# One decoder layer on one core: value slots a mix tile sooner, pairs of key pages summed on ScalarE, and five small steps moved

## What is computed

```
z  = x @ w_in                      columns q | k | v | B | C | h, 512 each
attention (8 heads x 64): block-sparse, ALiBi, over q, k, v
short convolution (512 channels): B * dwconv3_causal(C * h)
x1 = LayerNorm(alpha * x + concat(attn, conv) @ w_out)
u  = dwconv3_causal(x1 @ w_ffn_up);  a, g = split(u)
y  = LayerNorm(alpha * x1 + (silu(a) * g) @ w_ffn_down)
```

```
page_sum = sum over a page of cache_k[page_table]      -> block means -> gate -> top 3 blocks
p = softmax(q . k / 8 - slope * distance), other blocks masked;   out = p @ v
```

## Time and profile before

| | |
|---|---|
| median of three runs | 437.73 us |
| profiled execution | 437.8 us, its span 436.0 us |
| mean granted TensorE clock | 0.993 |
| TensorE busy | 412.7 us (95%) |
| VectorE busy | 294.7 us (68%) |
| ScalarE busy | 181.4 us (42%) |
| GpSimd busy | 110.8 us (25%) |
| DMA moved | 124.60 MB |

### The profile page before, as it was taken

The page is one execution under the profiler, slowest core; times in us unless marked ns, Lnnn a source line. Parts: engine busy times, 40 slices in busy tenths (PEclk is TensorE's granted clock), DMA queues, the critical chain, the costliest instruction groups (busy, mean ns, idle before and its releaser), DMA issues.

```text
span 436.0 us, 8237 instructions
## 1 busy us (share of the span) xinstructions
PE 412.7 (95%) x2903; PEld 339.2 (78%) x2903; DVE 294.7 (68%) x382; ACT 181.4 (42%) x694; POOL 110.8 (25%) x133
## 2 busy tenths in 40 slices
PE   4999999999999998999999989999999999999990
PEld 4588887876876774765653479999999999999990
DVE  0498999999799976954541275666776776534437
ACT  1587569644469133112110243554455555233201
POOL 1005334995255152200000717122211220000002
PEclk9999999999999999999999999999999999999997
DMA  8999999899999999999999953665556766676002
GB/s 313 397 359 407 405 407 393 316 404 409 409 359 327 338 404 405 406 405 404 402 405 398 318 196 98 194 191 162 158 169 191 213 181 186 183 211 206 3 2 99
DMA packets 109515, 124.60 MB, mean 286 GB/s; under 512 B 5903, under 2 KB 67048, under 8 KB 109466
## 3 DMA queue, kind: packets, MB, share of 16 engines
q1 hardware_dynamic: 101138, 107.30, 70.2%
q10 hardware_dynamic: 8336, 16.78, 10.2%
HBM read 121.65 MB, written 2.61 MB: 285 GB/s over the span
## 4 chain that ended last, share of the span: by engine, by line
PE 64%; DVE 18%; DMA 5%; issue 5%; SPq 4%; POOL 2%; ACT 1%; DVEq 0%; POOLq 0%; ACTq 0%
PE ps L1821 12%; PE ps L1822 11%; PE ps L1823 11%; PE ps L1714 8%; PE ps L1608 6%; DVE qk L939 6%; DVE T L949 5%; PE ps L1437 4%; PE ps L1632 4%; PE ps L1634 3%; PE ps L1384 3%; SPq L360 2%; DMA wring<-in_cache_v 2%; DMA KV<-in_cache_k 2%; POOL x1l L612 1%
## 5 line engine op out<-in xcount | busy, mean ns | idle before, releaser
L1188 DVE TENSOR_TENSOR wlo<-KV,whi 128x2048 fp32r<-128x2048 f32 (+1 forms) x24 | 61.7, 2571 | 57.5 <-ACT whi L838 29.3
L1437 PE MATMUL ps<-xT,wring 128*128 128x264 f32 x384 | 89.6, 388 | 0.1
L1437 PEld LDWEIGHTS ps<-xT,wring 128*128 128x128 f32 x384 | 71.6, 190 | 13.6 <-issue 1.7
L1821 PE MATMUL ps<-x1h,whi 128*128 128x264 f32 x256 | 73.7, 288 | 0.2
L1822 PE MATMUL ps<-x1l,whi 128*128 128x264 f32 x256 | 72.7, 284 | 0.0
L1823 PE MATMUL ps<-x1h,wlo 128*128 128x264 f32 x256 | 72.6, 284 | 0.0
L939 DVE TENSOR_TENSOR qk<-KV,qk 128x1536 f32<-128x1536 f32 (+1 forms) x32 | 67.0, 2097 | 6.6 <-DMA KV<-in_cache_k 2.7
L669 ACT ACTIVATE qk<-qk 128x64 f32<-128x64 f32 x216 | 51.9, 245 | 29.1 <-POOL qk L560 23.1
L949 DVE TENSOR_REDUCE T<-qk 128x24 f32<-128x1536 f32 (+1 forms) x32 | 58.4, 1827 | 0.0
L1821 PE MATMUL ps<-fh,whi 128*128 128x264 f32 x176 | 50.4, 286 | 0.1
L1822 PE MATMUL ps<-fl,whi 128*128 128x264 f32 x176 | 50.0, 284 | 0.0
(11 more groups left out here) (215 smaller groups left out, 574.0 us busy)
## 6 DMA issues: line engine op xcount, KB each, us to landing
KV<-in_cache_k SPq DMA_DIRECT2D x128, 256.0 KB, 6.2
KV<-in_w_ffn_up SPq DMA_DIRECT2D x32, 512.0 KB, 4.7
KV<-in_cache_v SPq DMA_DIRECT2D x60, 256.0 KB, 7.3
wring<-in_cache_v SPq DMA_DIRECT2D x56, 256.0 KB, 6.4
KV<-in_w_ffn_down SPq DMA_DIRECT2D x8, 1408.0 KB, 6.3
wring<-in_w_in ACTq DMA_DIRECT2D x5, 2048.0 KB, 14.0
zbuf<-in_cache_v SPq DMA_DIRECT2D x12, 256.0 KB, 5.3
zbuf<-in_w_ffn_up SPq DMA_DIRECT2D x3, 1024.0 KB, 10.2
```

The source lines that it names most:

```text
L1188: nc.vector.tensor_tensor(wlo[s][:, 0:n], w2[s][:, 0:n], whi[s][:, 0:n], ALU.subtract).then_inc(s_lo, 1)
L1437: ins = nc.tensor.matmul(ps[:, z_bank(n), 0:R], tile[k], xT[:, k, :], start=k == 0, stop=k == KT - 1)
L1821: nc.tensor.matmul(out, wh[k], xh[k], start=k == 0, stop=False)
```

## The change

Seven edits, each in the order or in the share of work of an engine:

- TensorE: `penalties(0)` stands in the middle of `z_tile(19)`, not ahead of it.
- TensorE: `values(0, 0)` stands ahead of the four transposes for the convolution's tail. Each later value slot up to `values(1, 3)` stands one mix tile sooner.
- GpSimd: page 17 is multiplied before the fourth convolution tile, not behind all four.
- VectorE: `multiply(20)` stands ahead of `denominators(0)`, and `scan(19)` becomes `reduce(19)`.
- Slots 22, 24, 26 and 28: VectorE sums two pages, not three, and ScalarE sums two, not one. The third page's products are VectorE's, so ScalarE can begin with them when VectorE's multiplication is done. VectorE's multiplications of slots 24, 26, 28 and 30 now also wait for ScalarE's sums of two slots before.
- SyncE: value slot 9 is fetched after the keys of sample 7's third group and a block of w_ffn_up, not before them.
- ScalarE: the copy `kv_rows(0)` stands ahead of `head_exp(0)`.

```diff
+HALVED = (22, 24, 26, 28)
@@ SyncE
             load_values(8, ids_v)
-            load_values(9, ids_v)
             load_keys(7, 2, ids_k)
             load_quad(1)
+            load_values(9, ids_v)
             load_keys(7, 3, ids_k)
@@ GpSimd
             for t in range(4):
+                if t == 3:
+                    multiply_page(17)
...
-            multiply_page(17)
             multiply_page(18)
@@ ScalarE, sum_products(j)
-                if j in POOLED:
-                    act.wait_ge(s_kpool, pool_pages(j + 1))
-                else:
-                    act.wait_ge(s_kused, j + 1)
-                for h in range(NH):
-                    x = prod[:, j % 2, GD * DA + h * DH:GD * DA + (h + 1) * DH]
...
+                for g in range(2 if j in HALVED else GD, GP):
+                    if g == GD and j in POOLED:
+                        act.wait_ge(s_kpool, pool_pages(j + 1))
+                    else:
+                        act.wait_ge(s_kused, j + 1)
+                    for h in range(NH):
+                        x = prod[:, j % 2, g * DA + h * DH:g * DA + (h + 1) * DH]
...
@@ ScalarE
+            kv_rows(0)
             head_exp(0)
-            kv_rows(0)
@@ VectorE, multiply(j) and reduce(j)
-                    if j not in POOLED:
+                    if j not in POOLED or j - 2 in HALVED:
                         dve.wait_ge(s_reda, act_sums(j - 1))
...
-                n = GP if j in WHOLE else GD
+                n = GP if j in WHOLE else 2 if j in HALVED else GD
@@ VectorE
             reduce(18)
+            multiply(20)
             denominators(0)
...
-            scan(19)
+            reduce(19)
@@ TensorE
-            penalties(0)
-            z_tile(19)
+            z_tile(19, lambda: penalties(0))
...
+            values(0, 0)
+            pe.wait_ge(s_ch, 4)
+            pe.wait_ge(s_hoc, 4)
+            for t in range(4):
+                ins = turn(ps[0:NTAIL, 3, t * P:(t + 1) * P], zT[:, 20 + t, TAIL:R])
+            ins.then_inc(s_ctps, 1)
             pe.wait_ge(s_wom, 16)
...
-            values(0, 0)
+            values(0, 1)
             mix_tile(0)
...
```

More of the change, by code:

```diff
@@ L1590, in _ @@
             head_outputs(3)
-            pe.wait_ge(s_ch, 4)
-            pe.wait_ge(s_hoc, 4)
-            for t in range(4):
-                ins = turn(ps[0:NTAIL, 3, t * P:(t + 1) * P], zT[:, 20 + t, TAIL:R])
-            ins.then_inc(s_ctps, 1)
             def values(b, s):
@@ L1656, in _ @@
             pe.wait_ge(s_ze, 24)
-            values(0, 0)
+            values(0, 1)
             mix_tile(0)
+            values(0, 2)
             mix_tile(1)
-            values(0, 1)
+            values(0, 3)
             mix_tile(2)
-            values(0, 2)
+            values(1, 0)
             mix_tile(3)
@@ L1665, in _ @@
             first_row_tile(0)
-            values(0, 3)
+            values(1, 1)
             mix_tile(4)
@@ L1669, in _ @@
             first_row_tile(2)
-            values(1, 0)
+            values(1, 2)
             mix_tile(5)
@@ L1673, in _ @@
             sample_outputs(0)
-            values(1, 1)
             mix_tile(6)
             first_row_tile(4)
-            values(1, 2)
+            values(1, 3)
             mix_tile(7)
@@ L1680, in _ @@
             first_row_tile(6)
-            values(1, 3)
             first_row_tile(7)
```

2 lines of the change are left out of this document (1 added, 1 removed).

## The result

| kernel | median of runs | ratio to before, 95% interval |
|---|---|---|
| before | 437.82 us (11 runs, 436.78 to 439.15) | 1 |
| changed | 438.73 us (11 runs, 437.74 to 440.26) | 1.0026, 1.0016 to 1.0037 |

The change makes the kernel 0.9 us longer by the medians; the ratio is estimated from all runs and puts it at 1.1 us, 0.7 to 1.6. The forecast was 436.5 us, with a range of 435.3 to 438.0: wrong in its sign, and outside its range.

The account below looks back on a forecast made before the run. The prediction took TensorE's list up to the last value slot at 239.40 us as the bound, with at most 1.42 us of DMA waits to win. +0.15 - 1.42 = -1.27 us gave 436.5 us, range 435.3 to 438.0.

Parts of the forecast that it names:

- term B: TensorE's waits for late value slots from 220 us on: all three go, -1.42 us, bounds 0 and -1.42.
- 2.0 us of lead stay: DMA behind the mix stretch: slot 20's latency of 6.2 us less slot 2's 4.2 was taken as lasting lead.
- reading M: Experiments' reading: slot 31 lands at slot 19's landing + 34.2 us or slot 20's issue + 38.4, whichever is later.
- term A: How much later TensorE leaves the mix stretch and row statistics: +0.15 us, bounds -0.24 and +2.4.
- waits for values 5 and 6: TensorE's mix stretch: value slots wanted a mix tile earlier are waited for, 0.2 us each, 0.4 us in all.
- take the place: Page 17 earlier on GpSimd: +0.3 us at 106 us, replacing the 0.4 us of waiting for values, adding nothing.
- Rival 1: Mix stretch: values arrive too late at a slower DMA rate, so the kernel is slower, 438.6 us; chance 0.13.
- rival 3: End of the value slots: the DMA's lead is lost, no waits go, 437.95 us; chance 0.15.
- the penalties' wait: TensorE's 0.86 us wait in the z tiles moves to the transpose of the maxima: 0, bounds 0 and -0.86.
- VectorE's new wait for ScalarE at slot 24: Multiplication of slot 24 waits for ScalarE's slot 22 until 133.6, ahead of its old time: 0 on the path.
- waits for the DMA at the end: Sign that the forecast is wrong: TensorE still waits for the DMA at the end; the forecast had none from 220 us.

Follow-up runs that it names:

- the block that fills the gap: Changed kernel with the 1 MB feed-forward weight block issued behind value slot 19, not slot 24: 436.92 us, 0.9979 of before.
- the control without a gap: Kernel before with the 1 MB feed-forward weight block issued behind value slot 19, not slot 24: 438.17 us, 1.0005 of before.
- the hole opened in the kernel before: Kernel before with two feed-forward half products put ahead of value slots 14 to 16 on TensorE: 444.88 us, 1.0162 of before.
- The same kernel without the block: Changed kernel with page 17, the four waits and values(1, 3) moved back, weight block still behind slot 24: 437.24 us, 0.9993 of before.
- the kernel with fillers: Kernel before with two keep_clock filler products (1.44 us) behind early_half(0, 0) on TensorE, run again: 439.72 us, one run.

## Why the prediction was wrong

- **The term B, -1.42 us, is the step that failed: "So 6.2 - 4.2 = 2.0 us of lead stay".** I read slot 20's latency against slot 2's and called the difference lead, to be used up at the end. By reading M the end of the profiled execution of before could gain 239.25 - 238.25 = 1.0 us at most, and in its second and third (200.19 + 38.4 = 238.6, landed 238.53; 200.81 + 38.4 = 239.2, landed 238.57) nothing; the size of a lead in one execution is no better known than the 38.4. Measured in the pair of first profiles, the length from slot 20's issue to slot 31's landing fell by 0.9 us (39.4 to 38.5), and slot 20's issue came 0.8 later. The prediction said itself that slot 20's "home waits for TensorE to use slot 14, which no edit moves". What follows from that was not drawn: sooner transfers ahead of slot 20 cannot bring it forward, they only let the queue run dry. Shown by the rates (404 to 280 GB/s), by the block that fills the gap (2.1 us back), by the control without a gap (last landing no sooner), and by the hole opened in the kernel before (7.2 us).
- **The term A was +0.15 and is +0.8 in the first profile (0.37 up to the transpose of the maxima and 0.43 behind it).** The waits for values 5 and 6, 0.4 us forecast, were nearly right in sum, though the trace shows only 0.17 of it as a wait, at 146.97: from the first mix tile to the row transposes it takes 37.46 us against 37.61 before, so -0.15 where -0.24 - 0.34 + 0.4 = -0.18 was reckoned. Too low was the start of the first tile (+0.58 against +0.34, for GpSimd's gate ahead of slot 1). And page 17's 0.2 to 0.4 us ahead of 106 us, for which 0.3 was reckoned, did not "take the place" of the waits for values, but came on top: that was the reckoning of A at fault. 0.22 of the 0.8 us is the difference at 90 us, within the spread of one kernel. Counted from VectorE's multiplication there to the use of slot 14, the kernel before takes 108.73 us in all three executions, the changed one 109.31 and 109.68: A is +0.6 and +0.95.
- **Rival 1's bounds do not agree with A's.** A was bounded at +2.4 "with the worst rate that the rows allow", but 2.4 us belongs to 3.0 us a slot; rival 1 itself has 3.8 us at 320 GB/s. Nothing of the outcome hangs on it.
- **The sum put right**: A passes on in full, since slot 14's use is what binds, and B is 0 or nearly: +0.8 + 0 = +0.8 us (+0.6 and +0.95 in the two executions), measured +0.9. The close agreement is in part luck: in the first pair of profiles slot 31 was used 0.11 us sooner than before. It is rival 3 with A at its real size; rival 3 gave 437.95, for it kept A at +0.15. Its condition ("other fetches fill the lead") was not what did it.
- **What held**: the DMA over 380 GB/s at 135 to 150 (404); rival 1's late values did not come; the penalties' wait moved and saved nothing; VectorE's new wait for ScalarE at slot 24 hid (134.08, forecast 133.6); keep_clock kept its length. Of the signs named for wrong, two came: waits for the DMA at the end, and row statistics later than 166.5 (166.56).
- **My theory Q of the experiments fell in part too.** It held that TensorE's tenths do not matter beside the queue. The same kernel without the block at 0.9993, and 1.36 us for 1.3 us of filler in the kernel before, show that they pass on whole. Slot 31 landing 40.4 us behind slot 20 in one kernel comes in part from slot 15's later use; what makes it 39.7 in another and 37.8 in a third, with a thin queue in both, stays open.

## What to carry to other kernels

Between a transfer that comes sooner and the end stands each buffer's next release: ask which fetch waits for a use that no edit moves, and take the path from there, not the total of idle transfer time. A lead read off one execution by the latency of one fetch can be gone in the next; a second profile of the kernel before would have shown it. To compare stretches of two executions, count from an instruction ahead of the edits: here the same stretch of one kernel came out at 108.73 us three times, while its start varied by 1 us. Where a gap in the queue can't be avoided, put into it a fetch whose place is free early: against the transpose of the maxima the last landing came 2.5 to 3.9 us sooner by a fetch of 2.6 us, and the end 0.9 to 2.6, as far as the landings still set it. A fetch put ahead of one that is soon needed can cost a wait, as in the control (2.20 us).

## What was not expected of the hardware

- A queue that runs thin moves less for longer than the gap itself. After the gap at 200 us the changed kernel's DMA share was back at 1.05, as in the full stretches, but 391 and 392 GB/s were moved in the next 20 us instead of 404; in the kernel with fillers 349 at a share of 0.95. With the block ahead it was 406 from 216 us on, and 401 in the kernel before from 216 to 226.
- TensorE's granted clock fell behind waits of a few us. It was 0.83 over 206 to 216 us behind one wait of 2.20 us, and 0.50, 1.2 GHz, over 216 to 226 behind waits of 1.91, 1.51 and 1.19 us; a half product of 3.6 to 3.7 us then took 5.41 and 5.32.
- The times of one kernel differ by up to 2.4 us (before: 436.78 to 439.15), and already at 106 us of the span by 1.0 us. One profile of each kernel would have said "no change" here (437.80 and 437.74); only the medians showed 0.9 us.
